# Norm of the second layer's keys and queries: squares summed on TensorE, late tiles of x updated between scaled tiles, a separate operand for the queries

## The reference, cut to what matters

```python
x = x + gate * (pooled @ a_w_out)                     # end of the pooling layer
n = x * rsqrt(mean(x * x, axis=-1) + 1e-6)            # one norm, two uses
hk = (n * kv_norm_g) * (1 + scale_kv) + shift_kv      # operand of keys and values
kv = hk @ w_kv                                        # 1024 x 1024 @ 1024 x 256
hb = (n * norm_g) * (1 + scale_b) + shift_b           # operand of queries and gate
q, z = split(hb @ b_w_in)                             # 1024 x 1024 @ 1024 x 2048
```

## Time and profile before

| | us |
|---|---|
| median of 3 runs | 2619.98 |
| the runs | 2614.60, 2619.98, 2620.13 |
| the profiled execution, its own time | 2616.37 |
| its span in the profile | 2614.1 |
| PE busy | 2491.4 (95%) |
| DVE, ACT, POOL busy | 1665.0, 950.2, 658.7 |
| stage `keys` up to b2 (from its first one-half product) | 2101.9 to 2220.2 |

### The profile page before, as it was taken

The page is one execution under the profiler, slowest core; times in us unless marked ns, Lnnn a source line. Parts: engine busy times, 40 slices in busy tenths (PEclk is TensorE's granted clock), DMA queues, the critical chain, the costliest instruction groups (busy, mean ns, idle before and its releaser), DMA issues.

```text
span 2614.1 us, 32078 instructions
## 1 busy us (share of the span) xinstructions
PE 2491.4 (95%) x12208; PEld 2052.8 (79%) x12208; DVE 1665.0 (64%) x2829; ACT 950.2 (36%) x1764; POOL 658.7 (25%) x536
## 2 busy tenths in 40 slices
PE   7899999888999899999999999999999998999998
PEld 5688888777887688888888877888877775888987
DVE  4699999476425877786644368476595566104843
ACT  5521212577123422222312244233243245225842
POOL 3167322576443000000000120000000044334753
PEclk9999999999999999999999999999999999999999
DMA  5112333001354365564623132232355123533242
GB/s 187 33 41 65 97 97 112 26 1 67 127 189 125 105 199 188 171 188 141 231 75 113 61 109 81 97 97 89 105 201 217 43 70 113 177 118 104 102 159 100
DMA packets 264323, 302.10 MB, mean 116 GB/s; under 512 B 11272, under 2 KB 216556, under 8 KB 264172
## 3 DMA queue, kind: packets, MB, share of 16 engines
q1 hardware_dynamic: 263860, 299.96, 35.1%
q10 hardware_dynamic: 312, 0.09, 0.0%
HBM read 228.15 MB, written 70.29 MB: 114 GB/s over the span
## 4 chain that ended last, share of the span: by engine, by line
PE 83%; DVE 10%; ACT 4%; issue 1%; DMA 1%; POOL 1%; SPq 0%; DVEq 0%; ACTq 0%; POOLq 0%
PE ps L67 81%; PE ps L70 2%; DVE tmp L79 1%; DVE sm L79 1%; ACT tmp L73 1%; DVE tmp L76 1%; ACT pth L73 1%; DVE wl L76 1%; DVE X L79 1%; DVE pwa L76 1%; DVE B2l L76 1%; DVE ptl L79 0%; DVE bl L79 0%; DVE pwb L76 0%; DVE ws L76 0%
## 5 line engine op out<-in xcount | busy, mean ns | idle before, releaser
L76 POOL TENSOR_TENSOR wl<-raw,wh 128x512 fp32r<-128x512 f32 (+1 forms) x224 | 293.4, 1330 | 1568.6 <-ACT wh L73 1568.4
L73 ACT ACTIVATE wh<-raw 128x512 fp32r<-128x512 f32 (+1 forms) x388 | 226.4, 621 | 243.6 <-PE ps L67 183.3
L67 PE MATMUL ps<-B2h,wh 128*128 128x512 f32 x616 | 244.1, 396 | 13.5 <-DVE B2l L76 7.0
L67 PE MATMUL ps<-B2l,wh 128*128 128x512 f32 x616 | 241.3, 392 | 0.0
L67 PE MATMUL ps<-B2h,wl 128*128 128x512 f32 x616 | 241.1, 391 | 0.0
L73 ACT ACTIVATE tmp<-ps 128x512 f32<-128x512 f32 (+5 forms) x163 | 118.2, 736 | 325.2 <-PE ps L67 313.9
L76 DVE TENSOR_TENSOR tmp<-tmp,ps 128x512 f32<-128x512 f32 x204 | 138.4, 685 | 109.0 <-PE ps L67 92.7
L67 PE MATMUL ps<-ah,wh 128*128 128x512 f32 (+1 forms) x608 | 192.5, 393 | 9.2 <-DVE al L76 5.0
L73 ACT ACTIVATE wh<-ws 128x512 fp32r<-128x512 f32 x152 | 94.3, 626 | 291.4 <-DVE ws L76 263.9
L67 PE MATMUL ps<-B3h,wh 128*128 128x512 f32 x448 | 178.3, 398 | 15.2 <-DVE B3l L76 7.1
L67 PE MATMUL ps<-ah,wl 128*128 128x512 f32 (+1 forms) x608 | 190.4, 390 | 0.0
(11 more groups left out here) (292 smaller groups left out, 5751.7 us busy)
## 6 DMA issues: line engine op xcount, KB each, us to landing
ada<-in_ada_w SPq DMA_DIRECT2D x48, 512.0 KB, 3.7
raw<-in_w_in SPq DMA_DIRECT2D x37, 512.0 KB, 4.4
raw<-in_a_w_in SPq DMA_DIRECT2D x33, 512.0 KB, 4.6
gates<-tmp SPq DMA_DIRECT2D x32, 512.0 KB, 3.0
raw<-in_w_ffn_gate SPq DMA_DIRECT2D x24, 512.0 KB, 5.9
hd<-tmp SPq DMA_DIRECT2D x22, 512.0 KB, 4.6
gf<-hd SPq DMA_DIRECT2D x22, 512.0 KB, 7.2
raw<-in_a_w_out SPq DMA_DIRECT2D x20, 512.0 KB, 3.4
```

Of the source, the lines that this page charges most:

```text
L67: return self.e.matmul(*a, **k) if self.e else Ins()
L73: return self.e.activation(*a, **k) if self.e else Ins()
L76: return self.e.tensor_tensor(*a, **k) if self.e else Ins()
```

## The change

- Squares: ACT writes the square of each X tile into a pair of half tiles; PE sums it over the features at once (4 matmuls with one column, into column 4j + i of a PSUM half), two products later. DVE no longer adds squares; it sums the eight columns with one `tensor_reduce`. The last two squares of h = 1 are summed inside k half 0.
- The updates of X2 to X7 in h = 1 stand among the tiles of pass (0, 0).
- The queries' operand has tiles `bh2`, `bl2` of its own: j = 0 to 5 in tiles free after "pl" (`b_place_free`), j = 6 and 7 in tiles of the keys' operand, free when the values are done. Four of its tiles for h = 0 are made before pass (1, 1), four after it. The ring `sc` has 5 half tiles.
- The evacuations of k and v and their copies come after the last pass; x's stores before. Tiles of later stages change places, and `sp_window` drops the wait for `QZ`.

```diff
+        self.bh2 = [m(f"bh2{j}", i, FR) for j, i in enumerate((4, 5, 6, 7, 0, 1, 16, 17))]
+        self.bl2 = [m(f"bl2{j}", i, FR) for j, i in enumerate((32, 33, 34, 35, 2, 3, 18, 19))]
...
-        self.n4 = five("n4", self.X)
+        self.n4 = Norm("n4", self.X, None, t[1], half(t[2]), half(t[3])[:1], half(t[3])[1:] + half(t[4]) + half(t[0]),
+                       order=[(p, j) for p, n in ((0, range(8)), (2, range(4)), (1, range(8)), (2, range(4, 8)), (3, range(8)))
+                              for j in n])
...
+    def pe_square1n(self, e, nm, h, j):
...
+        e.wait_ge(*self.at("sq", nm.name, h, j))
...
+        for i in range(4):
+            c = 4 * j + i
+            ins = e.matmul(p[:, c:c + 1], sq[:, 128 * i:128 * i + 128], self.ones[:, 0:1], start=True, stop=True)
...
 pe_keys:
+        def squares(h, j):
+            for i in {(1, 0): (6, 7), (1, 1): ()}.get((h, j), (8 * h + j - 2,)):
+                if i >= 0:
+                    self.pe_square1n(e, n4, i // 8, i % 8)
...
-                          {1: lambda: self.pe_sums(e, self.n4, 0), 2: lambda: self.pe_rstd(e, self.n4, 0)})
+                          {1: lambda: self.pe_rstd(e, n4, 0)}, each=squares)
+        self.pe_halves_of_two(e, ("k2", "v2"), [self.w8(self.A["w_kv_2"], 128 * i) for i in range(2)],
+                              self.by_norm(n4, self.bh, self.bl, (0, 1)),
+                              ({1: square(1, 6), 3: square(1, 7)}, {1: lambda: self.pe_rstd(e, n4, 1)}))
...
+    def b_place_free(self, j):
+
+        return [self.POOL_OUT] if j < 6 else [("prod", "v2")]
...
 act_keys:
+        self.act_scaled(e, n4, 0, 0, self.bh, self.md(48), [self.POOLED],
+                        hooks={0: square(2), 2: square(3), 3: four, 5: square(5), 7: six})
+        self.act_square1n(e, n4, 1, 7)
+        b0 = self.act_steps(e, n4, 2, 0, self.bh2, self.md(24), tiles=self.b_place_free)
+        next(b0)
+        self.act_sums(e, n4, 1)
+        for j in range(1, 4):
+            next(b0)
+        self.act_rstd(e, n4, 1)
         self.act_w(e, "v2", 4)
+        self.act_scaled(e, n4, 1, 1, self.bh, self.md(48), [self.POOLED])
+        for j in b0:
+            pass
+        self.act_w(e, ("b", 0), 4)
+        self.act_scaled(e, n4, 3, 1, self.bh2, self.md(24), tiles=self.b_place_free)
+        e.wait_ge(*self.at("prod", "v2"))
         e.activation(self.kx0[0:64, :], self.ps("k2")[0:64, :], ACT.Copy).then_inc(self.sig["evac"].up(("kx", 0)), 1)
...
 dve_keys:
+        update(1, 0)
+        self.dve_sums1n(e, n4, 0)
+        update(1, 1)
+        self.dve_scaled(e, n4, 0, 0, self.g3(2), self.bl, self.bh, self.md(48), [self.POOLED],
+                        hooks={0: later(2), 2: later(3), 3: later(4), 5: later(5), 7: later(6)})
+        update(1, 7)
+        b0 = self.dve_steps(e, n4, 2, 0, self.g3(1), self.bl2, self.bh2, self.md(24), tiles=self.b_place_free)
+        next(b0)
+        self.dve_sums1n(e, n4, 1)
+        for j in range(1, 4):
+            next(b0)
+        self.dve_scaled(e, n4, 1, 1, self.g3(2), self.bl, self.bh, self.md(48), [self.POOLED])
+        for j in b0:
+            pass
+        self.dve_scaled(e, n4, 3, 1, self.g3(1), self.bl2, self.bh2, self.md(24), tiles=self.b_place_free)
...
 pool_keys:
         self.pool_w(e, "k2", 4)
+        self.pool_scaled(e, self.n4, 2, 0, self.bl2, self.bh2, tiles=range(4))
         self.pool_w(e, "v2", 4)
         self.pool_scaled(e, self.n4, 1, 1, self.bl, self.bh)
-        self.pool_scaled(e, self.n4, 2, 0, self.bl, self.bh)
+        self.pool_scaled(e, self.n4, 2, 0, self.bl2, self.bh2, tiles=range(4, 8))
         self.pool_w(e, ("b", 0), 4)
+        self.pool_scaled(e, self.n4, 3, 1, self.bl2, self.bh2)
         self.pool_w(e, ("b", 1), 4)
-        self.pool_scaled(e, self.n4, 3, 1, self.bl, self.bh)
...
 sp_window:
-            if j == 1:
-                e.wait_ge(*self.at(*self.QZ))
-            else:
+            if j > 1:
                 e.wait_ge(*self.at("prod", ("s2", 4 * j - 5)))
             self.sp_queries(e, j)
```

More of the change, by code:

```diff
@@ L845, in sc_place, with act_square1n @@
     def sc_place(self, nm, p, j):
-        return 8 * p + j
+        return nm.order.index((p, j)) if nm.order else 8 * p + j
+    def act_square1n(self, e, nm, h, j):
+        c, i = slice(h * 512, h * 512 + 512), 8 * h + j
+        e.wait_ge(*self.at("sum", nm.name, h, j))
+        if i >= 2:
+            e.wait_ge(*self.at("prod", "sq", nm.name, (i - 2) // 8, (i - 2) % 8))
+        e.activation(nm.sq[i % 2], nm.X[j][:, c], ACT.Square).then_inc(self.sig["evac"].up(("sq", nm.name, h, j)), 1)
+    def pe_square1n(self, e, nm, h, j):
+        p = self.ps(("sums", nm.name, h)) if j else self.take(e, ("sums", nm.name, h), False)
+        e.wait_ge(*self.at("sq", nm.name, h, j))
+        self.takes += 1
+        for half in self.halves:
+            if half.before == [("sums", nm.name, h)]:
+                half.taken = self.takes
+        sq = nm.sq[(8 * h + j) % 2]
+        for i in range(4):
+            c = 4 * j + i
+            ins = e.matmul(p[:, c:c + 1], sq[:, 128 * i:128 * i + 128], self.ones[:, 0:1], start=True, stop=True)
+        ins.then_inc(self.sig["prod"].up(("prod", "sq", nm.name, h, j)), 1)
@@ L848, in lows, with dve_scaled, dve_steps @@
     def lows(self, p, j, shift):
         return "plo" if j % 2 else "vlo"
-    def dve_scaled(self, e, nm, p, h, g, lo, hi, shift=None, after=(), turned=False, hooks={}):
+    def dve_scaled(self, *a, hooks={}, **k):
+        for j in self.dve_steps(*a, **k):
+            if j in hooks:
+                hooks[j]()
+    def dve_steps(self, e, nm, p, h, g, lo, hi, shift=None, after=(), turned=False, tiles=None):
         c = slice(h * 512, h * 512 + 512)
@@ L873, in dve_scaled @@
                 s = nm.sc[i % len(nm.sc)]
-                for event in after:
+                for event in tiles(k) if tiles else after:
                     e.wait_ge(*self.at(*event))
@@ L884, in dve_scaled, with act_scaled, act_steps @@
                                            op0=ALU.add, op1=ALU.subtract).then_inc(self.sig["vlo"].up(*marks), 1)
+            yield j
+    def act_scaled(self, *a, hooks={}, **k):
+        for j in self.act_steps(*a, **k):
             if j in hooks:
                 hooks[j]()
-    def act_scaled(self, e, nm, p, h, hi, shift=None, after=(), hooks={}):
+    def act_steps(self, e, nm, p, h, hi, shift=None, after=(), tiles=None):
         c = slice(h * 512, h * 512 + 512)
@@ L897, in act_scaled @@
                 e.wait_ge(*self.at("shifted", nm.name, p, h, j))
-            for event in after:
+            for event in tiles(j) if tiles else after:
                 e.wait_ge(*self.at(*event))
@@ L903, in act_scaled, with pool_scaled @@
                 e.activation(hi[j][:, c], s, ACT.Copy).then_inc(done(("nhi", nm.name, p, h, j)), 1)
-            if j in hooks:
-                hooks[j]()
-    def pool_scaled(self, e, nm, p, h, lo, hi, hooks={}):
+            yield j
+    def pool_scaled(self, e, nm, p, h, lo, hi, hooks={}, tiles=range(NT)):
         c = slice(h * 512, h * 512 + 512)
-        for j in range(1, NT, 2):
+        for j in tiles[1::2]:
             i = self.sc_place(nm, p, j)
@@ L2058, in half_units, with dve_update @@
                     middle[j]()
-    def dve_update(self, e, nm, name, h, j, before, gate=None):
+    def dve_update(self, e, nm, name, h, j, before, gate=None, squares=True):
         c, X = slice(h * 512, h * 512 + 512), nm.X[j]
@@ L2072, in dve_update @@
                                    op1=ALU.add).then_inc(self.sig["vec"].up(*marks), 1)
-        if not nm.two:
+        if not nm.two and squares:
             self.dve_square(e, nm, j, h)
@@ L2849, in pe_keys, with pe_halves_of_two @@
                 self.gemm(e, ("b", j), self.unit(("b", j), self.w8(Wb, 128 * j)), h)
+    def pe_halves_of_two(self, e, keys, w8s, acts, hooks=({}, {})):
+        us = [self.unit(k, w) for k, w in zip(keys, w8s)]
+        for i in range(2):
+            self.gemm(e, keys[i], us[i], acts, (0,), hooks=hooks[i], end=False)
+        for i in range(2):
+            self.gemm(e, keys[i], us[i], acts, (1,))
+    def b_place_free(self, j):
+        return [self.POOL_OUT] if j < 6 else [("prod", "v2")]
     POOLED = ("prod", ("pool", 2, 7))
@@ L2857, in sp_keys @@
         self.sp_w(e, "v2")
[L2858 to L2862, removed]
         for j in range(NT):
@@ L2908, in act_keys, with four, six @@
             e.wait_ge(*self.at(*event))
[L2910 to L2917, removed]
-        self.act_w(e, "v2", 4)
[L2919 to L2924, removed]
+        n4 = self.n4
+        for j in range(NT):
+            if j % 2 == 0:
+                self.act_w(e, ("pl", "w", 0, j))
+            self.act_square1n(e, n4, 0, j)
+        self.act_w(e, ("pl", "w", 1, 0))
+        self.act_square1n(e, n4, 1, 0)
+        self.act_sums(e, n4, 0)
+        self.act_square1n(e, n4, 1, 1)
+        self.act_rstd(e, n4, 0)
+        self.act_w(e, ("pl", "w", 1, 2))
```

(20 more changed lines are left out.)

48 lines of the change are left out of this document (32 added, 16 removed).

## The result

Predicted were 2617.5 us: 2.5 us below the kernel before, too little to be told from no change. The changed kernel took a median of 2628.65 us (2626.79 to 2630.45, 6 runs), the kernel before beside it 2618.92 (6 runs): ratio 1.0038, 95% interval 1.0025 to 1.0051, so 9.7 us slower. The profiled execution took 2628.73, its span is 2626.5.

The account below looks back on a forecast made before the run. PE carries 83% of the chain; after the change the passes on DVE and POOL decide b2, at 2217.7 against 2220.18. So 2619.98 − 2.5 = 2617.5 us, range 2610.5 to 2623.

Parts of the forecast that it names:

- Cost 0, cover 0.8 for the second block; from below 0, from above 1: Evacuations behind the last pass: done 6.8 us after its last high part, PE at b2 after 7.6; cost 0.
- the slower rival: PE idles more before v half 1 and gets half clock: 2622.3 with 24 matmuls, 2627.1 with 48; chance 0.10.
- the end of 2623.0: High end of the time range: 1.27 us per meeting, 2620.6, and 12 matmuls at half clock, 2623.
- Squares at 0.95 a set: PE up to v half 0's end: 16 sets cost 15.2 us, offsetting removed idle and half clock; gain −0.7.
- R, then the passes: h = 1: R ready at 2170.7, 2.0 later; remaining passes end with POOL's last low part at 2211.4.
- What a meeting costs: Each POOL instruction beside DVE's scaled instructions costs DVE 1.05 us; 14 behind R, 14.7 us in all.
- the rival: Passes: each meeting costs DVE POOL's whole 1.27 us, 3.1 more in all, time 2620.6; chance 0.07.
- QZ: Fetch of queries 1: SP's queue order holds it, so dropping the wait gains 0, between 0 and 0.3.
- The gain of 2.5 without the bank: Stage before b2: b2 starts at about 2217.7 instead of 2220.18, 2.5 us earlier; the bank was not considered.
- half clock rival: v half 1, b0's last step, b1 half 1: 0.2 us per half-clock matmul, gain gone from 13; chance 0.10.

Follow-up runs that it names:

- experiment 6: Changed kernel, sums' bank not marked newly taken by the last two square sets, wait for QZ put back before the fetch of queries 1: 2615.71 us, one execution.
- experiment 1: Changed kernel, but the sums' bank is not marked as newly taken by the last two square sets: 2618.39 us, ratio 1.0.
- experiment 5: Changed kernel, sums' bank unmarked at last two square sets, b0's weights made before second half's sums, b1's between queries' tiles 5 and 6: 2614.7 us, ratio 0.9987.
- experiment 10: The kernel before, unchanged, profiled once more: 2615.89 us, one execution.
- experiment 3: Kernel before, with only the evacuations of keys and values, their copies and b2's weights moved behind the last pass: 2627.08 us, ratio 1.003.
- experiment 7: Changed kernel, sums' bank unmarked at last two square sets, every set of squares summed twice: 2633.36 us, ratio 1.0059.

## Why the prediction was wrong

**The step that failed** is "Cost 0, cover 0.8 for the second block; from below 0, from above 1" for the evacuations behind the last pass. It costed them as work for ACT that must be done before b2, and did not ask which products before b2 need the bank that they free. It measured 13.1 us of wait and some 1.6 of half clock behind it; the stage is 12.4 longer than forecast. The earlier trace rows held the hint. The evacuation of k, from 2193.57 to 2195.61, was early for b2, but PE stood before b1 half 0 from 2196.43 on, and only the wait for weights kept it until 2198.68:

```profile
2198.68 0.77 PE L67 MATMUL ps<-bh,wh 128*128 128x512 f32 x1 [2.25 <-POOL wl L76]
```

So the dependence had 3.1 us of cover. The evacuation moved back by 16.3, counted from the stage's start, and the difference is the wait of 13.1 within 0.2. The bank can be read in `take()` and in `pe_square1n`, for both kernels. Neither the slower rival nor any other had this wait. With the bank repaired the same change takes 2618.39, inside the range; this wait alone carried it beyond the end of 2623.0.

Of the other steps, counted from the stage's start (2.2 us later after):

- Squares at 0.95 a set: the sets at 2112.26 and 2115.93 are 3.67 apart, as the updates in the join stage. Doubled sets cost 0.88 by the time, 0.89 by the updates. v half 0 ends 71.5 behind the start, as forecast. **Right.** The loss there is 1.4 and not 0.7, since v half 0 ended at 2172.0 before: the idle stretch from 2172.7 lies inside k half 1.
- R, then the passes: R at 2170.7 + 2.2 = 2172.9 was forecast, DVE starts on it at 2172.56. It stands at tile 6 after 19.8 us, where 19.7 was forecast, and waits 4.23 instead of 3.9. POOL's last low part ends at 2213.54 (2212.28 and 1.26), 109.4 behind the start, where 109.5 was forecast. **Right in the sum, in part by luck.** The last low part of pass (1, 1) came 15.3 us after R (2172.56 to 2187.85) instead of 16.7, since the three additional POOL instructions put it off by 1.8 together and not 3.15. Eight matmuls at half clock from 2187.11, which the sum had at nothing, then held back the values, and with them tile 6, by some 1.6. Without them, in experiment 6, ACT writes tile 6 at 90.4 behind the start instead of 91.8 in experiment 1, and the last low part ends at 108.3.
- What a meeting costs: 1.03 where it can be read cleanly on DVE (experiment 5), so the 1.05 was **right** there; what it costs a pass depends on where POOL's instructions fall. By the Trainium skill ("SBUF — State Buffer", SBUF: two separate sides) "the other fully blocks"; read as in the rival, with DVE paying POOL's whole 1.27, three would cost 3.8, and no row here shows that. Where POOL's instructions follow each other, DVE's pair of scaled instructions takes 3.15 and POOL's take 1.71 each. Full blocking in turn would be 0.67 + 1.27 = 1.94 for one of each, so both sides are slowed, but not by the whole of the other.
- QZ: **right**, PE waits 3.58 after and 3.39 before.
- The gain of 2.5 without the bank: **not found in the time.** Experiment 1's kernel, with experiment 6, gives stages of 117.7, 117.7, 117.6 and 114.7, before 118.3 and 116.7, where 115.8 was forecast. Without half clock the stage is 114.7, and two stretches put 3 us on it. That is the prediction's own half clock rival, at 16 matmuls ("From 13 matmuls on the gain is gone"). One stretch is where it said, at b0's last step and b1 half 1, the other a little earlier, in the last steps of k half 1. It was given a tenth and came in three executions of four. The argument against it was one quiet stretch of before, 2172.7 to 2182.4; in experiment 10 the same kernel has half clock from 2181.7 on, where that stretch ends. And the prediction's list of half clock before left out the stretch from 2160.8 to 2167.5.

## What to carry to other kernels

When an evacuation is moved, list which bank each later product takes, by the rule that hands them out, and date the evacuation by the first product that takes its bank, not by the unit that reads the result. Where buffers are handed out by last use, an edit that only refreshes a mark moves every wait behind it. A dependence that shows no wait may still have little cover: here it had 3.1 us, 2.25 of them a wait for weights, and the move turned it into a wait of 13.1.

Work brought onto a full engine pays in full (0.9 us a set), and what it removes from others is worth only the idle time it closes. What helped here was to put small works of POOL and ACT where DVE waits anyway (experiment 5).

## What was not expected of the hardware

The same instructions with the same short waits in front of them got different clocks. At b0's last steps PE waits 1.14 and 0.89 us in experiment 1, 1.15 and 0.88 in experiment 6. Behind these waits it ran at 0.51 in the one and at 1.00 in the other. In this stage a wait of 3.6 us or more was followed by half clock each time (3.62 and 3.63 in the two executions of before, 3.62 in experiment 3, there 1.3 us behind it, 13.10, 13.47). In experiment 7 the clock fell without any idle time, while PE summed 32 records of one column, and twelve matmuls behind them ran at half clock. What decides behind the short waits stays open. For a forecast, a stage with such waits has a spread of its own, here 3 us.
